# A two-block network on one core: router transposes moved behind the logits, a ninth 2 MB home for expert weights, and the first pair's tokens gathered one expert at a time

## What is computed

```python
def expert_choice_ffn(h, w_router, w_gate, w_up, w_down):
    bn, seq, dm = h.shape
    cap = CAPACITY_FACTOR * seq // N_EXPERTS          # 2 * 512 // 16 = 64
    probs = jax.nn.softmax(jnp.einsum('bld,de->ble', h, w_router).astype(jnp.float32), axis=-1)
    scores = jnp.transpose(probs, (0, 2, 1))
    gate, idx = lax.top_k(scores, cap)
    xs = jax.vmap(lambda hb, ib: hb[ib])(h, idx)
    a = jnp.einsum('becd,edf->becf', xs, w_gate)      # each weight: 1024 x 2048
    u = jnp.einsum('becd,edf->becf', xs, w_up)
    y = jnp.einsum('becf,efd->becd', jax.nn.silu(a) * u, w_down)
    y = (y * gate[..., None]).astype(h.dtype)
    ...                                               # y added back to its tokens

def first_block(x, ...):
    ...
        x = x + (merged @ w_out[l]).astype(x.dtype)
        h2 = rms_norm(x, norm2_g[l])
        x = x + expert_choice_ffn(h2, w_router[l], w_gate[l], w_up[l], w_down[l]).astype(x.dtype)
    return rms_norm(x, final_g)
```

## Time and profile before

| what | value |
|---|---|
| median of 3 runs | 1819.38 us (1818.92 to 1820.71) |
| profiled execution, its own time | 1819.85 us |
| its span in the trace | 1818.1 us |
| granted TensorE clock, mean over the span | 0.988 |
| PE busy | 1716.2 us (94%) |
| DVE / ACT busy | 658.4 us (36%) / 439.4 us (24%) |
| HBM read | 487.49 MB, 269 GB/s over the span |

### The profile page before, as it was taken

How to read it: one execution, slowest core, us unless ns; L and a number is a source line. 1 busy time by engine, 2 the same in 40 slices (tenths; PEclk the granted TensorE clock), 3 DMA queues, 4 the chain that set the end, 5 groups by cost and what they waited for, 6 DMA issues and landing times.

```text
span 1818.1 us, 20416 instructions
## 1 busy us (share of the span) xinstructions
PE 1716.2 (94%) x8778; PEld 1055.0 (58%) x8778; DVE 658.4 (36%) x921; ACT 439.4 (24%) x554; POOL 0.2 (0%) x4
## 2 busy tenths in 40 slices
PE   7999999999898997989989889899999999999998
PEld 7888875343332432424324243287878888888886
DVE  8995623011010110100101001057645565746645
ACT  5434320110000100101001010055343343323333
POOL 0000000000000000000000000000000000000000
PEclk9999999999999999999999999999999999999999
DMA  6236438999999999999999999980512222222311
GB/s 204 94 91 212 155 132 353 430 433 430 432 433 430 433 429 434 431 433 433 428 436 428 434 430 432 426 305 5 178 54 93 89 93 96 93 92 92 116 47 47
DMA packets 63243, 492.56 MB, mean 271 GB/s; under 512 B 6096, under 2 KB 10192, under 8 KB 48592
## 3 DMA queue, kind: packets, MB, share of 16 engines
q1 hardware_dynamic: 63184, 491.70, 66.5%
HBM read 487.49 MB, written 2.10 MB: 269 GB/s over the span
## 4 chain that ended last, share of the span: by engine, by line
PE 77%; DMA 17%; DVE 4%; issue 1%; ACT 1%; SPq 0%; DVEq 0%
PE ps L481 21%; PE ps L457 19%; PE ps L1306 16%; PE ps L1318 10%; DMA xd<-w_up 10%; PE ps L616 3%; DMA xd<-w_down 3%; PE ps L628 3%; DMA raw<-w_in 2%; DMA xd<-w_gate 2%; PE ps L1186 1%; PE ps L1355 1%; DMA xin<-x_t 1%; DVE lo L427 1%; PE ps L1673 0%
## 5 line engine op out<-in xcount | busy, mean ns | idle before, releaser
L1306 PE MATMUL ps<-xd,xe 128*64 128x512 f32 x2048 | 465.3, 607 | 52.9 <-DMA xd<-w_up 28.1
L1306 PEld LDWEIGHTS ps<-xd,xe 128*64 128x64 f32 x2048 | 146.3, 140 | 363.8 <-issue 286.9
L1318 PE MATMUL ps<-xd,hidT 128*64 128x512 f32 x960 | 217.9, 607 | 5.4 <-ACT hidT L1441 3.4
L1568 DVE TENSOR_TENSOR hid<-hid,ps 128x512 f32<-128x512 f32 x32 | 20.6, 684 | 536.5 <-PE ps L1306 536.5
L427 DVE TENSOR_TENSOR lo<-raw,hi 128x2048 fp32r<-128x2048 f32 x72 | 162.6, 2259 | 142.6 <-ACT hi L418 139.8
L418 ACT ACTIVATE hi<-raw 128x2048 fp32r<-128x2048 f32 x71 | 134.2, 1890 | 177.4 <-PE ps L481 82.7
L481 PE MATMUL ps<-xh,hi 128*128 128x512 f32 x416 | 164.9, 396 | 1.3 <-DVE ga L1029 1.3
L481 PE MATMUL ps<-xl,hi 128*128 128x512 f32 x416 | 162.3, 390 | 0.0
L457 PE MATMUL ps<-xh,hi 128*128 128x512 f32 x384 | 149.9, 390 | 0.0
L457 PE MATMUL ps<-xl,hi 128*128 128x512 f32 x384 | 149.4, 389 | 0.0
L1318 PEld LDWEIGHTS ps<-xd,hidT 128*64 128x64 f32 x960 | 73.1, 139 | 129.2 <-issue 125.6
(11 more groups left out here) (450 smaller groups left out, 1775.6 us busy)
## 6 DMA issues: line engine op xcount, KB each, us to landing
xd<-w_down SPq DMA_DIRECT2D x28, 4096.0 KB, 27.0
xd<-w_gate SPq DMA_DIRECT2D x28, 4096.0 KB, 29.4
xd<-w_up SPq DMA_DIRECT2D x26, 4096.0 KB, 28.3
raw<-w_in SPq DMA_DIRECT2D x24, 1024.0 KB, 8.2
xd<-w_up SPq DMA_DIRECT2D x12, 2048.0 KB, 15.2
raw<-ffn_up_w SPq DMA_DIRECT2D x24, 1024.0 KB, 5.0
xd<-w_gate SPq DMA_DIRECT2D x8, 2048.0 KB, 11.0
raw<-ffn_down_w SPq DMA_DIRECT2D x12, 1024.0 KB, 5.1
```

What stands on the lines that cost most here:

```text
L1306: mm = pe.matmul(ps[64 * half:64 * half + 64, bank + b, :], xe[:, k, CAP * u:CAP * (u + 1)], xs[n % NXS][:, f:f + 512], start=(k == 0), st ...
L1318: mm = pe.matmul(ps[64 * nn:64 * nn + 64, YB, :], hidT[:, 4 * (c % 2) + kk, CAP * half:CAP * (half + 1)], xs[n % NXS][:, kk * D + nn * 512 ...
L1568: tt(hid[:, 512 * b:512 * b + 512], hid[:, 512 * b:512 * b + 512], ps[:, UB + b, :], ALU.mult) \
```

## The change

1. The four groups of transposes that stood in chunk 19 now stand behind the logits, so that all 32 transposes are there. They go through four PSUM banks instead of two. ACT copies all eight groups after the softmax's exponential. The fillers are 30 instead of 26, and the wait for the last copy stands ahead of `idm`'s matmul. DVE makes the indices with one instruction fewer (a predicated copy).
2. All tiles start 15.5 KB lower in SBUF (`BASE`, and a smaller scratch for dynamic DMAs). In the room at the top lies `x8`, a ninth home of 2 MB. It takes piece 7, which is loaded during the mixer, ahead of pieces 4 and 5. Piece 15, whose home is thereby free from the start, is loaded where 7 was. After that `x8` isn't used again.
3. In the first pair the gathers make 64 columns (one expert) at a time: expert 0's at the old places, expert 1's behind the `down` pieces of expert 0 (chunks 0 and 1 behind the first, 2 and 3 behind the second, 4 to 7 behind the third). ACT copies 64 columns at a time there, and the counts of `xe_done` and `gx_ps` move by four.

```diff
-    nc = bacc.Bacc("TRN2", target_bir_lowering=False, num_devices=1)
+    nc = bacc.Bacc("TRN2", target_bir_lowering=False, num_devices=1, dynamic_dma_scratch_size=512)
...
-        BASE = 16512
+        BASE = 640
...
+        x8 = at("x8", [P, XCH], F32, 207)
...
-        def gather(pe, k, each=False):
-
-            o = ps[:, TB + k // 2 % 2, (k % 2) * P:(k % 2 + 1) * P]
+        def gather(pe, k, each=False, c0=0, nc_=P):
+
+            o = ps[:, TB + k // 2 % 2, (k % 2) * P + c0:(k % 2) * P + c0 + nc_]
...
-                mm = pe.matmul(o, htk[:, t, k * P:(k + 1) * P], s1[:, t, :], start=(t == 0), stop=(t == NT - 1))
+                mm = pe.matmul(o, htk[:, t, k * P:(k + 1) * P], s1[:, t, c0:c0 + nc_], start=(t == 0), stop=(t == NT - 1))
...
-        LB, SB, HB, IB = 0, 1, (2, 3), 4
+        LB, SB, HB, IB = 0, 1, (2, 3, 5, 7), 4
...
-            chunk_mms(pe, 19, QQ, 0, 4, xh, xl, closes=False, after={(0, 1): first_turned, (1, 1): last_turned})
+            chunk_mms(pe, 19, QQ, 0, 4, xh, xl, closes=False)
...
-            turned(0, 1)
-            turned(1, 1)
+            for t in range(NT):
+                turned(t, 0)
             pe.wait_ge(sem("pr_done"), 1)
...
-            turned(2, 1)
-            turned(3, 1)
-
-            keep_busy(26, 2 * P)
+            for t in range(NT):
+                turned(t, 1)
+
+            keep_busy(30, 2 * P)
+            pe.wait_ge(sem("hth_done"), 2 * NT)
             pe.wait_ge(sem("idm_done"), 1)
...
-            pe.wait_ge(sem("hth_done"), 2 * NT)
...
-            gather(pe, 0, True)
-            gather(pe, 1)
-            gather(pe, 2)
+            gather(pe, 0, True, nc_=CAP)
+            gather(pe, 1, nc_=CAP)
+            gather(pe, 2, nc_=CAP)
...
                         down(c)
+                        if u == 0 and first and c < 3:
+                            for k in ((0, 1), (2, 3), (4, 5, 6, 7))[c]:
+                                if k >= 4 and k % 2 == 0:
+                                    pe.wait_ge(sem("xe_done"), k // 2 + 3)
+                                gather(pe, k, c0=CAP, nc_=CAP)
...
-            for t in range(NT):
-                take_turned(t, 1)
+            for half in range(2):
+                for t in range(NT):
+                    take_turned(t, half)
...
+                    if u == 0 and first:
+                        for q in range(4):
+                            take_xe(q, q + 5, c0=CAP, nc_=CAP)
...
-            ts(other[:, 0, :], idx[32:32 + NE, ::-1], float(SEQ // 2), None, ALU.add)
+            dve.tensor_copy(other[:], top[32:32 + NE, ::-1])
             dve.tensor_copy(mine[:], idx[0:NE])
-            L(dve.tensor_copy(other[:, 1, :], top[32:32 + NE, ::-1]))
-            tt(mine[:], mine[:], other[:, 0, :], ALU.subtract)
-            L(tt(pick_a[:], top[0:NE], other[:, 1, :], ALU.is_ge))
-            L(tt(mine[:], mine[:], pick_a[:], ALU.mult))
-            L(tt(iv2[:, 0, 0:CAP], mine[:], other[:, 0, :], ALU.add))
+            L(ts(iv2[:, 0, 0:CAP], idx[32:32 + NE, ::-1], float(SEQ // 2), None, ALU.add))
+            L(tt(pick_a[:], top[0:NE], other[:], ALU.is_ge))
+            L(dve.copy_predicated(iv2[:, 0, 0:CAP], pick_a[:], mine[:]))
...
-                if n >= NXS:
+                if n >= NXS and n != 2 * NXS - 1:
                     sp.wait_ge(sem("xs_used"), n - NXS + 1)
...
+            load_half(NXS - 1)
             sp.wait_ge(sem("uz_done"), 4)
             load_half(4)
             load_half(5)
...
-            for n in (2, 3, 6, 7, *range(NXS, 2 * NXS)):
+            for n in (2, 3, 6, 2 * NXS - 1, *range(NXS, 2 * NXS - 1)):
                 load_half(n)
```

More of the change, by code:

```diff
@@ L279, in build @@
         idx = at("idx", [48, CAP], U32, B + 47.25)
[L280 removed]
+        other = at("other", [NE, CAP], F32, B + 47.5)
         mine = at("mine", [NE, CAP], F32, B + 48)
[L282 removed]
+        pick_a = at("pick_a", [NE, CAP], U32, B + 48.25)
         iv2 = at("iv2", [NE, 2, P], F32, B + 49)
@@ L594, in x_arrived @@
         def x_arrived(pe, n, i):
-            base = 16 if n % NXS >= 6 else 0
+            base = 16 if n == 6 and isinstance(i, int) and i == 0 else 0
             if n % NXS < 4 and not (isinstance(i, int) and i == 0 and n < 2 * NXS):
@@ L1300, in up @@
                             x_arrived(pe, n, i)
+                        extra = first and u == 0 and n == NXS - 1
+                        if extra:
+                            pe.wait_ge(sem("x8_in"), 16)
+                        piece = x8 if extra else xs[n % NXS]
                         for kk in range(2):
@@ L1331, in pair @@
                                 if j:
-                                    gather(pe, k)
+                                    gather(pe, k, nc_=CAP)
                             pe.wait_ge(sem("xe_done"), j + 1)
@@ L1402, in take_turned @@
                 a(htk[:, t, 512 * half:512 * half + 512].rearrange("p (k m) -> p k m", k=4),
-                  ps[:, HB[t % 2], :].rearrange("p (m k) -> p k m", k=4), ACT.Copy).then_inc(sem("hth_done"), 1)
+                  ps[:, HB[(4 * half + t) % len(HB)], :].rearrange("p (m k) -> p k m", k=4), ACT.Copy).then_inc(sem("hth_done"), 1)
             def square(k):
@@ L1419, in experts_act, with take_xe @@
             a(lg, lg, ACT.Exp).then_inc(sem("lge_done"), 1)
-            for t in range(NT):
-                take_turned(t, 1)
-            def take_xe(q, turn):
+            for half in range(2):
+                for t in range(NT):
+                    take_turned(t, half)
+            def take_xe(q, turn, c0=0, nc_=P):
                 act.wait_ge(sem("gx_ps"), turn)
                 for k in (2 * q, 2 * q + 1):
-                    last = a(xe[:, k, :], ps[:, TB + q % 2, (k % 2) * P:(k % 2 + 1) * P], ACT.Copy,
+                    last = a(xe[:, k, c0:c0 + nc_], ps[:, TB + q % 2, (k % 2) * P + c0:(k % 2) * P + c0 + nc_], ACT.Copy,
                              scale=prm[:, P_GX + k:P_GX + k + 1])
@@ L1509, in experts_dve @@
             tt(idm[:, 0:2, :], blocks[:, 0:2, :], wide.to_broadcast([NE, 2, CAP]), ALU.mult).then_inc(sem("idm_done"), 1)
-            L(tt(iv2[:, 1, 0:CAP], top[0:NE], other[:, 1, :], ALU.max))
+            L(tt(iv2[:, 1, 0:CAP], top[0:NE], other[:], ALU.max))
             for r in range(2):
@@ L2362, in load_half @@
                 k = rows.shape[1] // 2
-                d(xs[n % NXS].rearrange("p (k n) -> p k n", k=k), rows[:, k * (m % 2):k * (m % 2) + k, :]) \
-                    .then_inc(signal(n), 16)
+                home = x8[:] if n == NXS - 1 else xs[n % NXS]
+                d(home.rearrange("p (k n) -> p k n", k=k), rows[:, k * (m % 2):k * (m % 2) + k, :]) \
+                    .then_inc(sem("x8_in") if n == NXS - 1 else signal(n), 16)
             def load_x(m, i=0):
```

30 lines of the change are left out of this document (12 added, 18 removed).

## The result

| | median of 20 runs | range | ratio to before |
|---|---|---|---|
| before | 1819.68 us | 1818.60 to 1821.75 | |
| after | 1823.01 us | 1822.02 to 1825.57 | 1.0019 [1.0013, 1.0026] |

The change costs 3.3 us, 0.19%. The forecast was +2.3 us to 1821.7, inside a range of 1815.0 to 1824.5, and the same as before within what a measurement can tell. The size is small, but the interval of the ratio leaves 1 out: twenty runs on each side do tell 0.19% from nothing.

A forecast was written before the change was run, and what follows sets the result against it. The expert stage was taken as bound by its DMA weight stream. Later issue of pieces 20 and 21 moved their bytes from 356.5 to 358.8 us: 1819.38 + 2.3 = 1821.7 us, range 1815.0 to 1824.5.

The forecast's parts named there:

- the ninth home's 4.9 us: Expert weight stream: piece 7 comes in the mixer, so 2.1 MB less after the restart, 4.88 us if no later load is late.
- The sum: Whole kernel: +2.3 us on the median of 1819.38 gives 1821.7 us, counted as the same; chance 0.56.
- Transposes and scores: Router: logits and scores 1.6 us earlier; with 30 fillers at full clock only 0.3 us reaches the experts.
- Narrow gathers: First pair's gathers: 64 columns cost 0.116 us a row, the same as 128, so gathering expert by expert doubles the price.
- the second rival: Gathers: half the columns at half the price (0.066 us a row), -4.3 us to 1815.1 us; chance 0.12.
- PE's time to pieces 20 and 21: Ahead of that load: 7.5 us more from 64 extra gather rows and turns; issue moves from 350.67 to 357.4 us.
- the gathers' waits: Up to the first piece and between gathers: 0.24 us of waiting at four places, 0.5 us gained in all.
- the third rival: Clock falls ahead of the fillers as before: 1.6 us more, 1823.3 us, or 1824.3 with copy waits; chance 0.12.
- The clock behind the fillers: Router to first experts: clock forecast at 1.00 from 270 to 290 us; a fall considered only ahead of the fillers.
- the margin of 4.4 us: Load of pieces 20 and 21: could have begun at 352.1, began at 356.5 us; the stream can't get further ahead.
- the first rival: Expert stream: the ninth piece pays in full, -5.3 us to 1814.1 us, needing that load issued by 349.8; chance 0.09.
- The early load: Piece 7 in the mixer: hidden by about 5 us of cover; rival that PE waits at chunk 14: 1826, chance 0.03.

The follow-up runs named there:

- second execution: Second profiled execution of the changed kernel itself, nothing further altered: 1821.87 us.
- experiment 4: The kernel before with the gathers expert by expert alone; 1823.49 us, ratio 1.0026.
- experiment 5: The kernel before with the ninth home and 8, 8 and 16 idle 64-column matmuls where the change gathers for expert 1, gathers as before; 1823.08 us, ratio 1.0019.
- experiments 3 and 4: 3: the kernel before with the router's part alone, 1819.27 us, ratio 1.0001; 4: with the gathers expert by expert alone, 1823.49 us.
- first execution: First profiled execution of the changed kernel itself, one of its 20 runs: 1824.65 us.
- experiment 2: The kernel before with the ninth home alone (`x8`, `BASE` and the order of loads); 1817.97 us, ratio 0.9990.
- experiment 1: The changed kernel with the first pair's gathers as before (128 columns, both experts at once, old places); 1818.27 us, ratio 0.9992.
- experiment 6: The changed kernel with 24 fillers instead of 30; 1822.26 us, ratio 1.0011.

## Why the prediction was right, and where it was off

The mechanism held: gathering expert by expert costs PE 64 rows more ahead of pieces 20 and 21, their load goes out later than the stream could have taken it, and the ninth home's 4.9 us become holes. What was off is the base that the +2.3 us were added to (see The sum). By its steps:

- **Transposes and scores.** Forecast 1.6 us earlier; 1.8 in the second execution, levelled (271.68 + 0.45 against 273.91). The sixteen behind the scores take 1.80 us, not 2.1, so the fillers begin at 274.5, levelled, instead of 275.0. `idm` is ready at 285.2 (forecast 285.5; DVE's program has lost two instructions, seven against five, and not one as the description of the change says), fillers end at 287.5 (288.1), the first piece starts at 291.64 (292.1). That is a gain of 0.9 us instead of 0.45. But what it was gained on is the half clock in the fillers of the execution that I read: without that, experiment 4 shows the same start from the old router.
- **Narrow gathers.** 0.116 to 0.121 us a row, forecast 0.116. The transposes' 0.066, the second rival, is excluded by the change's own rows and by experiment 5's. By the Trainium skill's "TensorE: Matmul & The Clock Gate", section "LDWEIGHTS (loading the stationary operand)", a load of 128 columns takes about 107 ns (an estimate by its formula), and the rows agree. The table of its section "Back-to-back issue gap", from which the prediction took 134 and 60 cycles, is for a matmul by itself, and the spacing here did not fall as it has it when the streamed columns went from 128 to 64. The same section says that in a stream of loads and matmuls both set the spacing, which the rows bear out; so the page did not speak for the second rival as the prediction has it.
- **PE's time to pieces 20 and 21.** From the first piece to the issue before 350.67 - 292.55 = 58.1 us, now 357.07 - 291.19 = 65.9: 7.8 more, forecast 7.15 (7.5 - 0.35). The half a microsecond that I hoped to win on the gathers' waits is not there. Issue, levelled, 357.5 us; forecast 357.4. Two misses of half a microsecond cancelled, by luck.
- **The sum.** +2.3 forecast, +2.5 in the trace against the execution that I worked from, +3.3 in the medians. The forecast takes the fillers' half clock out of the kernel after (0.3 us from the router rest on it) and leaves it in the kernel before, and then adds the difference to a median. That execution restarted its stream 1.1 us late for it, as experiments 3 and 4 show. With full clock on both sides the change costs about 3.6 us. The prediction's own numbers would have given this: without the half clock 26 fillers end before `idm` is ready, and the first piece before starts near 291.5 instead of 292.55 us. How often each kernel's timed runs have a fall is not on record. In the profiled executions the fillers ran in part at half clock in 3 of 5 with the old router (PE's gap ahead of the scores 1.77 us in all five) and in none of 9 with the new one (0.90 us); so the fall of the third rival never came there, and the choice of full clock in the fillers, made for the shorter gap, held.
- **The clock behind the fillers.** I asked only whether it falls ahead of them, and wrote 1.00 from 270 to 290 us. It was 1.00 there, and fell at 291. A fall ahead of the first piece delays the restart in either kernel. Behind it, the kernel before has a margin of about 0.9 to 4.4 us at every load up to piece 20, which hides all or part of a fall; in the changed kernel PE has none at piece 20. The first execution's fall cost its full 1.7 us. How much such falls add to the medians stays open, as no timed run other than the profiled ones shows its clock by stretch.
- **The margin.** The sentence "the margin of 4.4 us is what decides" was true of pieces 20 and 21 alone. Piece 16 had 1.8 (issue 333.50 + 1.4 = 334.9 against 336.7), from a row that I had copied and not worked through. (Piece 10, issued at 305.25 us, had even less, 307.5 - 306.65 = 0.9, but the ninth home changes the order only behind piece 14.) It didn't alter the forecast, as the later hole is the larger one (the bytes of piece 16 would be 1.85 us early, those of 20 are 2.4 late). It did alter what the first rival needed, and made my expectation for experiment 2 miss by a factor of three, and that for experiment 1 by more.
- **The early load** was hidden: in experiment 2, which has it and the old router, the stream restarts at 296.20 us, levelled 296.31, against 296.25.

## What to carry to other kernels

A stream of loads into a ring of homes has a margin at every load: when its home was freed plus the start-up time (1.4 us here), against when its bytes could begin. Before adding a home or moving work on the engine that frees them, work it out for every load that the edit moves and take the smallest; the time at the end then moves by the one load that comes latest against its old time. Levelled, this is within about 0.3 us of the trace in eleven of the thirteen other profiled executions here; the two that it misses, by 1.0 and 1.8 us, are those of experiment 1's kernel in which PE's own work ended the stage. Here a float32 matmul with 128 weight columns got no cheaper when its streamed columns went from 128 to 64, so splitting the gather by columns doubled its price. And before a difference is counted from one profiled execution, see whether its clock fell on the path that the difference runs through: here it had fallen in the execution before, and so the +2.5 us between two traces understate what the change costs.

## What the runs showed of the hardware

- A float32 matmul with 128x128 weights costs 0.116 to 0.121 us a row with 64 streamed columns (the change, experiment 5) and 0.118 with 128. Loads with one streamed column follow each other every 0.116 us, so the price is that of the load; with 256 streamed columns a row takes 11.39 / 52 = 0.219 us (the fillers of experiment 4).
- The lower clock can come while PE is busy all the time: at 291.7 us in the change's first execution, after 16.99 busy us of the 17 from 274 to 291, and in experiment 6, where the last gap is 0.3 us at 286 us, from 290.2 to 297 us. Other falls stand behind a gap or in it: in the second execution of the change PE was idle from 1155 to 1157 us, and the clock was 0.50 from 1157 to 1160. The same program has a given fall in one execution and not in the next. I had expected it only behind a gap of PE.
- The first long run of chunks, ahead of anything that the change touches, starts between 77.74 us (experiment 5) and 79.91 us (experiment 6). In the change's first two executions, 1.04 us apart there, the first input landed at 14.17 and 13.08 us. This spread of 2.2 us is two thirds of the effect studied.
